# Experts' gate and up products with the weights stationary and the tokens moving

## What is computed

```
hg = jnp.einsum('td,edf->tef', t, w_gate)
hu = jnp.einsum('td,edf->tef', t, w_up)
hid = jax.nn.silu(hg) * hu * gates[:, :, None].astype(hg.dtype)
out = jnp.einsum('tef,efd->td', hid, w_down)
```

## Time and profile before

| | |
|---|---|
| median of 3 runs | 2016.2 us (2013.27 to 2019.76) |
| profiled execution | 2006.76 us |
| its span, first to last instruction | 2004.9 us |
| mean granted TensorE clock | 0.854 |
| PE busy | 1475.8 us, 74% |
| PEld busy | 1062.3 us, 53% |
| DVE busy | 700.2 us, 35% |
| ACT busy | 462.5 us, 23% |

### The profile page before, as it was taken

One profiled execution on the slowest core, in us unless ns is written; L12 is line 12 of the kernel. 1 busy time (PEld: TensorE's weight loads), 2 busy tenths in 40 slices (PEclk: granted clock), 3 DMA queues, 4 the chain that ended last, 5 costly groups with the idle time before them and its releaser, 6 DMA issues. The chain is left out here.

```text
span 2004.9 us, 25197 instructions
## 1 busy us (share of the span) xinstructions
PE 1475.8 (74%) x10086; PEld 1062.3 (53%) x10086; DVE 700.2 (35%) x1205; ACT 462.5 (23%) x802; POOL 226.6 (11%) x322
## 2 busy tenths in 40 slices
PE   3799788845699878398369888615996738988752
PEld 0799544411599633298245444315996725544431
DVE  2422256522227375812531111154244362111106
ACT  1322255511125431400301000023222230100012
POOL 2000133300000143200011110030002001111011
PEclk7899899877799688599679999857997967999985
DMA  6122587288222502210939999730221285999962
GB/s 258 42 84 85 227 303 294 106 335 339 68 84 67 213 1 91 88 64 21 362 128 388 384 393 401 262 131 23 91 98 45 63 341 189 386 394 396 393 235 98
DMA packets 133567, 399.58 MB, mean 199 GB/s; under 512 B 15826, under 2 KB 67666, under 8 KB 110674
## 3 DMA queue, kind: packets, MB, share of 16 engines
q1 hardware_dynamic: 114354, 359.01, 47.6%
q10 hardware_dynamic: 11488, 21.24, 2.9%
q0 software_dynamic: 7616, 17.84, 2.8%
HBM read 368.72 MB, written 37.19 MB: 202 GB/s over the span
## 5 line engine op out<-in xcount | busy, mean ns | idle before, releaser
L2370 PE MATMUL ex_gups<-ex_gu,ex_he 128*64 128x256 f32 x2048 | 252.7, 403 | 63.7 <-DMA ex_gu<-in_moe_w_up 60.7
L2370 PEld LDWEIGHTS ex_gups<-ex_gu,ex_he 128*64 128x64 f32 x2048 | 151.0, 145 | 146.9 <-DMA ex_gu<-in_moe_w_up 67.9
L2415 DVE TENSOR_TENSOR ex_hid<-ex_sg,ex_gups 128x128 f32<-128x128 f32 x64 | 18.4, 288 | 314.9 <-ACT ex_sg L2439 314.9
L224 PE MATMUL sc_ps<-h_hi,sc_hi 128*128 128x272 f32 x384 | 111.3, 290 | 21.5 <-PEq L1911 21.5
L2388 PE MATMUL ex_yps<-ex_dn,ex_hid_t 128*64 128x512 f32 x512 | 123.9, 604 | 0.9 <-issue 0.9
L2348 POOL DMA_INDIRECT ex_hg<-h_rows,route_tok x64 | 60.2, 941 | 517.2 <-PE ex_trps L2360 424.8
L224 PE MATMUL sc_ps<-h_hi,sc_w_r 128*128 128x272 f32 x384 | 111.1, 289 | 0.0
L224 PE MATMUL sc_ps<-hT_r,sc_hi 128*128 128x272 f32 x384 | 110.9, 289 | 0.0
L224 PE MATMUL xbcz_ps<-mixT_r,xbcz_hi 128*128 128x272 f32 x320 | 93.4, 292 | 16.3 <-DVE xbcz_w_r L321 16.3
L224 PE MATMUL xbcz_ps<-mixT_r,xbcz_w_r 128*128 128x272 f32 x320 | 93.0, 291 | 0.0
L224 PE MATMUL xbcz_ps<-hT_r,xbcz_hi 128*128 128x272 f32 x320 | 93.0, 291 | 0.0
(11 more groups left out here) (427 smaller groups left out, 3251.0 us busy)
## 6 DMA issues: line engine op xcount, KB each, us to landing
ex_gu<-in_moe_w_gate SPq DMA_DIRECT2D x64, 1024.0 KB, 25.2
ex_gu<-in_moe_w_up SPq DMA_DIRECT2D x64, 1024.0 KB, 26.0
ex_dn<-in_moe_w_down SPq DMA_DIRECT2D x64, 1024.0 KB, 25.9
ada_rest_w<-in_ada_w SPq DMA_DIRECT2D x40, 1024.0 KB, 7.0
as_pages<-in_cache_kT SPq DMA_DIRECT2D x32, 512.0 KB, 5.9
as_pages<-in_cache_v SPq DMA_DIRECT2D x32, 512.0 KB, 5.3
y_rows<-ex_yo ACTq DMA_DIRECT2D x128, 128.0 KB, 7.2
qkv_w<-in_mix_w_in SPq DMA_DIRECT2D x12, 1024.0 KB, 5.2
```

Source lines behind the costliest of these rows:

```text
L224: last = nc.tensor.matmul(ps[:, h, 0:HALF], w[:, j, f], x(j)[:, cols], start=(j == 0 and n == 0), stop=(j == kt - 1 and n == 2))
L2370: last = nc.tensor.matmul(gu_ps[64 * q:64 * q + 64, :, :], he[n % 2][:, j, :], ex.gu[n % S][:, :, j, q * P:(q + 1) * P], start=(j == 0), s ...
L2415: nc.vector.tensor_tensor(hid[:, :], sg[:, :], gu_ps[:, 1, :], ALU.mult).then_inc(done["hid"], 1)
```

## The change

In the main pass over experts, gate and up swap their operands. The weights are now stationary, 128 rows by 128 columns, and the 64 tokens move. For each part (gate, up), half q and slice j there is one product: 2 times 2 times 8 = 32 per expert, and in the trace 64 weight loads and 64 matmuls. The result has the features on the partitions and the tokens in the columns, which is the layout that the down product wants. So `turn_hidden`, its DVE copy and their two semaphores go away. DVE writes the gated values alternately into the two buffers that were `hid` and `hid_t`. It waits for the down product of two experts before (`done["y"]`), where it waited for the transpose. The down product waits for `hid` in place of `ht`.

```diff
-        done = {n: k.sem(f"{nm}a{n}") for n in ("tr", "he", "gu", "sg", "hid", "htp", "ht", "y", "yo")}
+        done = {n: k.sem(f"{nm}a{n}") for n in ("tr", "he", "gu", "sg", "hid", "y", "yo")}
...
-                for j in range(KT):
+                for part in range(2):
                     for q in range(2):
-                        last = nc.tensor.matmul(gu_ps[64 * q:64 * q + 64, :, :], he[n % 2][:, j, :],
-                                                ex.gu[n % S][:, :, j, q * P:(q + 1) * P],
-                                                start=(j == 0), stop=(j == KT - 1), skip_group_check=True)
+                        for j in range(KT):
+                            last = nc.tensor.matmul(gu_ps[:, part, q * CAP:(q + 1) * CAP],
+                                                    ex.gu[n % S][:, part, j, q * P:(q + 1) * P], he[n % 2][:, j, :],
+                                                    start=(j == 0), stop=(j == KT - 1))
                 last.then_inc(done["gu"], 1)
-
-            def turn_hidden(n):
-                pe.wait_ge(done["hid"], n + 1)
-                if n >= 1:
-                    pe.wait_ge(done["ht"], n)
-                nc.tensor.transpose(ht_ps[:, :], hid[:, :], k.ident[:, :]).then_inc(done["htp"], 1)
 
             def down(n):
                 pe.wait_ge(ex.dn_ready[n % S], 16 * (n // S + 1))
-                pe.wait_ge(done["ht"], n + 1)
+                pe.wait_ge(done["hid"], n + 1)
...
-                turn_hidden(n)
...
-                if n >= 1:
-                    dve.wait_ge(done["htp"], n)
-                nc.vector.tensor_tensor(hid[:, :], sg[:, :], gu_ps[:, 1, :], ALU.mult).then_inc(done["hid"], 1)
+                if n >= 2:
+                    dve.wait_ge(done["y"], n - 1)
+                nc.vector.tensor_tensor(hidden[n % 2][:, :], sg[:, :], gu_ps[:, 1, :], ALU.mult).then_inc(done["hid"], 1)
                 if n + 1 < NE:
                     keep_tokens(n + 1)
-                dve.wait_ge(done["htp"], n + 1)
-                if n >= 1:
-                    dve.wait_ge(done["y"], n)
-                nc.vector.tensor_copy(hid_t[:, :], ht_ps[:, :]).then_inc(done["ht"], 1)
```

More of the change, by code:

```diff
@@ L2325, in phase_experts @@
         hid_t = sb("hid_t", [P, P])
+        hidden = (hid, hid_t)
         yo = [sb(f"yo{b}", [P, 512]) for b in range(2)]
@@ L2387, in down @@
                     for c in range(2):
-                        last = nc.tensor.matmul(y_ps[n % 2][64 * c:64 * c + 64, :], hid_t[:, m * CAP:(m + 1) * CAP],
-                                                ex.dn[n % S][:, m, c * 512:(c + 1) * 512],
+                        last = nc.tensor.matmul(y_ps[n % 2][64 * c:64 * c + 64, :],
+                                                hidden[n % 2][:, m * CAP:(m + 1) * CAP], ex.dn[n % S][:, m, c * 512:(c + 1) * 512],
                                                 start=(m == 0), stop=(m == 1), skip_group_check=True)
```

## The result

| | before | changed |
|---|---|---|
| median | 2014.74 us (4 runs, 2010.56 to 2019.76) | 2198.83 us (4 runs, 2190.71 to 2202.77) |
| span of the profiled execution | 2004.9 us | 2198.6 us |
| mean granted clock | 0.854 | 0.85 |
| PE busy, records | 1475.8 us, 10086 | 1722.7 us, 12070 |
| PEld busy | 1062.3 us | 1397.8 us |

The ratio is 1.0907, with a 95% interval of 1.0866 to 1.0949: 9% slower. The forecast was 160 us more on the median of 2016.2; it became some 183 us more.

A forecast was written before the change was run, and what follows sets the result against it. PE bounds each loop first, then the weight stream; after the change PE throughout. Two loops of 329.5 us plus 18 us at the start make 695 against 535.3 us: +160, median 2176 us, range 2130 to 2400.

The forecast's parts named there:

- What bounds the kernel before: Two expert loops, 535.3 us: PE while the slots loaded ahead last, then the weight stream at 8.36 us per expert.
- the saved transpose: In each expert's step, the change removes one transpose of the gated values, 0.26 us on PE.
- Loads set the pace: Gate and up: 64 loads of 128 columns, 0.111 us apart, hide the streaming; 7.10 us per expert, 3.49 more.
- The serial rival: Gate and up: load and matmul one after the other, 0.167 us per record, 2405 us in all; chance 0.07.
- The rival of fast loads: Gate and up: loads as fast as a transpose's, 139 ns long, pace 0.060 us, time unchanged at 2015 us; chance 0.05.
- The start of each loop: Low clock until the first down product has run, two gate and up at 13.6 us each; 18 us per loop.
- the forecast's sum: Two loops of 329.5 + 18 = 347.5 us give 695 us against 535.3, +160 us; median 2176 us.
- its third rival: Low clock stays: gate and up lose it each time, 2684 us; partial loss lies between; chance 0.14, a third below 2400.
- a fall of the clock within the loop: Sign of being wrong: in the loops the clock should be low until some 30 us after the start, 1.00 afterwards.
- What would have shown it: Signs in the loops: loads 0.19 us long, 0.11 apart; step 10.3 us; no up-weight waits after the start; DMA share 0.75.

The follow-up runs named there:

- two runs that made PE's step shorter: Kernel before without the transpose of the gated values and its copy: 2013.88 us; changed kernel with weight loads of 64 columns in place of 128: 2012.88 us.
- The padded kernel: Changed kernel with every gate and up product moving 128 columns, 64 tokens plus 64 columns nobody reads: 2158.42 us, ratio 1.0732 to the kernel before.

## Why the prediction was right, point by point

**What bounds the kernel before.** PE for the first part of a loop, the weight stream after it. Shown by two runs that made PE's step shorter, by 0.4 us and by some 1.4 us, and left the time within about 0.4% of the kernel before. In the old loop the saved transpose is thus worth nothing measurable. In the changed loop, where PE sets the pace, it should still keep its 0.26 us out of each step; no run separates that.

**Loads set the pace.** Right. The loads start 0.112 us apart, forecast 0.111 from L1225. Halving their columns brought the time back to 2013 us; doubling what streams under them cost nothing. Gate and up measured 7.29 us against 7.10: 64 x 0.112 = 7.17 and some 0.12 more up to the start of the next kind of product, a hand-over that the sum had left out. The 0.19 us are 12 us over 64 experts.

**The serial rival.** Refuted by the changed kernel itself, 0.112 against 0.167 us, and more strictly by 128 moved columns at 7.34 us. The rule of the Trainium skill, TensorE: Matmul & The Clock Gate, on which the prediction draws for this rival stands in the section The mechanism, and taken by itself it is not borne out here: loads overlap matmuls though both use all rows of the array. The same section of the Trainium skill also lets a load be pulled ahead when it goes to the background weight buffer, which would fit; no run here shows that buffer.

**The rival of fast loads.** Refuted: the median load of gate and up (L2372) is 192 ns, not 139.

**The start of each loop.** Right in kind: the clock rose with the first down product. From 1036.48 to 1071.03 are 34.55 us, where full clock would give 2 x 7.29 + 2 x 1.37 + 1.87 = 19.2, so 15.4 us (15.6 in the second loop) against 18 taken, 5 us too much over both loops. Some 0.9 of the 15.4 is not the clock: the second gate and up starts 2.32 us behind the first transposes, not 1.37, with 0.83 us of idle time. In the code it waits there for the copy of its tokens, and no down product covers that yet; the profile names no releaser. The padded kernel has the same 0.83 us at full clock.

**The term that was missing.** The low clock was priced as a thing of the start or of every step. In fact it came back for one down product in six or so, behind the token transposes: 5 times in the first loop, at 1.65 us each. In the second loop it was 4 times, and that loop is 1.5 us shorter. Nine times 1.65 is 15 us.

The sum then closes: 695 + 12 - 5 + 15 = 717 us, measured 716.9. The three misses, +12, -5 and +15, are the 22 us by which the forecast was low, so its closeness owes little to errors that cancel. The step that failed is thus the one for the clock within the loop: the forecast's sum put it at nothing, and its third rival, which allowed for a loss in a part of the steps, gave that no price. The prediction named a fall of the clock within the loop as a sign of being wrong, and by that sign it was wrong in this term; the term is small, 15 of 182 us. That the clock is what costs these terms is shown by the padded kernel: with the same loads and the same order on PE, the falls vanish and the low clock at the start costs some 1.4 us in the first loop and 1.6 in the second. Why the clock falls at some transposes and not at others stays open; no run was made for it.

**What would have shown it.** Loads 0.19 us long and 0.11 apart, no waits for weights, DMA share 0.72 (some 0.75 forecast), step 10.52 us (10.3): as written. The clock at 1.00 after the start: no, it fell nine times.

No version beat the kernel before. The runs say why: with the old products the loop is at the rate of its weight stream, and anything that spares PE shows up as waiting.

## What to carry to other kernels

When choosing which operand is stationary, count loaded columns as well as streamed ones: in these runs a product took the longer of the two, and 128 loaded columns took as long as streaming 128 float32 columns (0.112 us against half of 0.226), so with 64 moving columns under 128 loaded ones the streaming stands still half of the time. Before taking work off an engine, look at what the step waits for last: one transpose per expert, removed alone, changed nothing. And where loads set the pace, useless moving columns can pay: here they cost 0.05 us per expert, kept the clock at 1.00 and made the kernel 35 us faster.

## What the hardware showed that was not expected

- More streaming was faster and less was slower, at equal loads: 32, 64 and 128 moving columns gave 2548, 2199 and 2160 us.
- Keeping and raising the clock are different things. Gate and up with 64 moving columns ran for 7 us at 1.00 after a stretch at 1.00, and for 13.8 us at 0.50 after a stretch at 0.50, in the first two steps of both loops. PE was busy throughout each of them.
- Products of 64 loaded and 64 moving columns ran at 0.040 us per record in the mean, although within one column half they start 0.056 us apart.
